# The mask of windowed attention added by a matmul with the identity instead of by VectorE

## The reference, cut to what matters

```
s_loc = einsum(q * scale, keys of 3 blocks)          # 128 queries x 384 keys
s_ctx = einsum(q * scale, context keys)              # 128 x 256
mask  = (|si - 128 - qi| <= 128) & (0 <= kpos < n)
s_loc = where(mask, s_loc, -inf)
p     = softmax(concat(s_loc, s_ctx, sink))
out   = p[:, :384] @ values of 3 blocks + p[:, 384:640] @ context values
```

## Time and profile before

| | us |
|---|---|
| median of 3 runs | 3833.14 |
| lowest, highest | 3831.15, 3833.17 |
| profiled execution, its own time | 3832.59 |
| its span in the profile | 3830.8 |
| TensorE busy in the span | 3366.6 |
| VectorE busy in the span | 1906.8 |

### The profile page before, as it was taken

The page is one execution under the profiler, slowest core; times in us unless marked ns, Lnnn a source line. Parts: engine busy times, 40 slices in busy tenths (PEclk is TensorE's granted clock), DMA queues, the critical chain, the costliest instruction groups (busy, mean ns, idle before and its releaser), DMA issues. The chain is left out here.

```text
span 3830.8 us, 47701 instructions
## 1 busy us (share of the span) xinstructions
PE 3366.6 (88%) x17144; PEld 2788.7 (73%) x17144; DVE 1906.8 (50%) x2918; ACT 847.1 (22%) x1570; POOL 1386.0 (36%) x1032
## 2 busy tenths in 40 slices
PE   0969989887979999999997669989787799999997
PEld 0848878755858888888884548878666578888885
DVE  8988533678582222222228888534675532222125
ACT  1136432212031010000003226432211121010102
POOL 1354213243324333343432253212242344444443
PEclk9979999978989999999998789999988899999998
DMA  7400001002301111011101510011002111111111
GB/s 276 170 17 1 1 29 60 12 20 85 121 28 39 39 38 38 33 44 39 35 30 67 176 55 1 0 39 50 12 14 80 39 39 49 49 49 50 44 49 49
DMA packets 63856, 197.72 MB, mean 52 GB/s; under 512 B 6160, under 2 KB 16656, under 8 KB 62736
## 3 DMA queue, kind: packets, MB, share of 16 engines
q1 hardware_dynamic: 54736, 172.32, 13.1%
q10 hardware_dynamic: 9024, 24.14, 1.7%
HBM read 177.05 MB, written 19.40 MB: 51 GB/s over the span
## 5 line engine op out<-in xcount | busy, mean ns | idle before, releaser
L188 PE MATMUL ps<-h_hi,f_whi 128*128 128x512 f32 (+1 forms) x1760 | 650.8, 370 | 27.0 <-DVE h_lo L1914 20.0
L189 PE MATMUL ps<-h_lo,f_whi 128*128 128x512 f32 (+1 forms) x1760 | 649.9, 369 | 0.0
L190 PE MATMUL ps<-h_hi,f_wlo 128*128 128x512 f32 (+1 forms) x1760 | 649.0, 369 | 0.0
L2142 DVE TENSOR_TENSOR f_gated<-f_gated,ps 128x512 f32<-128x512 f32 (+1 forms) x110 | 69.6, 634 | 973.8 <-PE ps L190 968.5
L2026 POOL TENSOR_TENSOR f_whi<-f_wraw,small 128x1024 fp32r<-128x1024 f32 x128 | 252.0, 1969 | 607.9 <-PE ps L190 607.9
L2150 DVE SCALAR_TENSOR_TENSOR x_res<-ps,mod,x_res 128x512 f32<-128x512 f32 (+1 forms) x440 | 306.8, 697 | 242.2 <-PE ps L190 242.0
L188 PEld LDWEIGHTS ps<-h_hi,f_whi 128*128 128x128 f32 x1760 | 333.2, 189 | 86.2 <-issue 22.7
L190 PEld LDWEIGHTS ps<-h_hi,f_wlo 128*128 128x128 f32 x1760 | 333.1, 189 | 55.7
L189 PEld LDWEIGHTS ps<-h_lo,f_whi 128*128 128x128 f32 x1760 | 333.4, 189 | 55.2
L188 PE MATMUL ps<-f_ahi,f_whi 128*128 128x512 f32 (+1 forms) x880 | 328.2, 373 | 0.0
L189 PE MATMUL ps<-f_alo,f_whi 128*128 128x512 f32 (+1 forms) x880 | 323.6, 368 | 0.0
(11 more groups left out here) (216 smaller groups left out, 6223.7 us busy)
## 6 DMA issues: line engine op xcount, KB each, us to landing
f_wraw<-in_w_ffn SPq DMA_DIRECT2D x132, 512.0 KB, 3.2
ada_w<-in_w_ada SPq DMA_DIRECT2D x80, 512.0 KB, 3.3
wrawc<-in_w_in SPq DMA_DIRECT2D x26, 512.0 KB, 3.7
wrawab<-in_w_in SPq DMA_DIRECT2D x16, 512.0 KB, 4.2
wrawo<-in_w_out SPq DMA_DIRECT2D x16, 512.0 KB, 3.3
ada_w<-in_w_ada ACTq DMA_DIRECT2D x16, 512.0 KB, 4.3
x_res<-in_xT SPq DMA_DIRECT2D x8, 640.0 KB, 6.3
x_spill<-x_res ACTq DMA_DIRECT2D x8, 640.0 KB, 5.9
```

The lines of the kernel that those rows point to most:

```text
L188: pe.matmul(out, w_hi, h_hi, start=first, stop=False)
L189: pe.matmul(out, w_hi, h_lo, start=False, stop=False)
L190: return pe.matmul(out, w_lo, h_hi, start=False, stop=last)
L2142: dve.tensor_tensor(g, g, pl.bank(3 + c, tn), ALU.mult).then_inc(u_taken[c], 1)
```

## The change

Two tiles are added at 188 KB and 188.5 KB of the stage's memory: the identity and the three masks, both in float32r. ScalarE fills them once per layer by copies from the constants, between the rounding of the first keys and the first exponential. TensorE opens each local unit's window with a matmul of identity (weights) and mask (moving, 384 columns) that starts the accumulation; the score matmuls of the window then accumulate on it. VectorE's addition and its semaphore wait are gone. TensorE waits for the two copies ahead of unit 0 alone.

```diff
+    ident = pl.at(f"{tag}_ident", [P, P], F32R, kb=188)
+    masks = pl.at(f"{tag}_masks", [P, 3, 3 * P], F32R, kb=188.5)
+    mask_in = pl.sem(f"{tag}_mask_in")
...
-                    pe.matmul(out, q_two[:, w.h, :], hi, start=True, stop=False)
-                    mm = pe.matmul(out, q_pad[:, w.h, :], lo, start=False, stop=True)
+                    local = w.kind == "A" and place < 3
+                    if local and place == 0:
+                        if w.static and w.u == 0:
+                            pe.wait_ge(mask_in, 2)
+                        variant = 1 if not w.static else 0 if w.i == 0 else 2 if w.i == LT - 1 else 1
+                        pe.matmul(w.scores(0, 3), ident[:, :], masks[:, variant, :], start=True, stop=False)
+                    pe.matmul(out, q_two[:, w.h, :], hi, start=not local, stop=False)
+                    mm = pe.matmul(out, q_pad[:, w.h, :], lo, start=False, stop=not local or place + n == 3)
...
-                if w.kind == "A":
-                    if w.static:
-                        variant = 0 if w.i == 0 else 2 if w.i == LT - 1 else 1
-                    else:
-                        variant = 1
-                    win = w.scores(0, 3)
-                    dve.tensor_tensor(win, win, pl.c(MASKS + 3 * P * variant, 3 * P), ALU.add) \
-                        .then_inc(masked, 1)
-                    dve.wait_ge(masked, w.u + 1)
...
             round_keys(0)
+            act.activation(ident[:, :], pl.c(IDENT), ACT.Copy).then_inc(mask_in, 1)
+            act.activation(masks[:, :, :].rearrange("p v k -> p (v k)"), pl.c(MASKS, 9 * P), ACT.Copy) \
+                .then_inc(mask_in, 1)
             exponent(Unit(0, 0, 0))
```

## The result

| | before | after |
|---|---|---|
| median, us | 3833.07 (6 runs) | 3812.89 (6 runs) |
| lowest to highest, us | 3831.15 to 3833.46 | 3806.95 to 3815.01 |
| profiled execution, us | 3832.59 | 3815.01 |
| its span, us | 3830.8 | 3813.2 |

The ratio after to before is 0.9948, with a 95% interval of 0.9938 to 0.9959: 20.2 us less in the median, 17.6 in the span of the profiled executions. A second series gave 3813.07 against 3832.03, ratio 0.9957 (0.9943 to 0.9971). I had forecast 3825.2 us, 7.9 less, in a range that ended at 3820.

What follows compares the result with a forecast made beforehand. The bound was taken as a cycle through TensorE and VectorE in the local attention units. Steps saving 9.5 us, less 1.6 lost at stage starts, gave 7.9 us off the median: 3825.2 us, range 3820 to 3833.

Steps and rivals of the forecast that it cites:

- What bounds the kernel: Local attention units: a cycle through TensorE and VectorE, 5.31 us for two units, the addition 0.60 of it.
- M: TensorE's cost of one added mask matmul of 384 columns: 0.175 us taken, bounds 0.16 and 0.26.
- rival 1: Mask matmul on TensorE: identity's load or opener's gap is paid, M = 0.26, saving 2.0 us, 3831.1 us; chance 0.15.
- The 53 steps: Unit-to-unit steps of both layers' local units at 2.4 GHz: 129.9 us against 139.3, 9.5 us saved.
- The copies at nothing: ScalarE's two added copies per layer: costed at nothing, at most their 1.4 us per layer.
- Start of each stage ... Net 1.6 us lost: Early units of each layer's attention: masks cost 16 M = 2.8 us, exposed first additions give 1.2 us back.
- One unit earlier or later in each layer is worth 3.3 us either way, and I can't tell which: TensorE's clock rise among each layer's early units: a one-unit shift is worth 3.3 us, direction unknown.
- The main case: The forecast itself, whole kernel: 7.9 us saved, 3825.2 us; chance 0.50.
- Rival 3: Early attention units: clock rises a unit earlier in both layers as TensorE idles less, 3.3 us more saved, 3821.9; chance 0.17.
- Rival 2: Local units: TensorE binds already and the addition was covered, so masks cost 12.1 us, 3845.2 us; chance 0.06.
- Rival 4: Ahead of the transposes: small waits of 0.08 us per unit stay, 4.2 us given back, 3829.4 us; chance 0.12.

Runs made afterwards that it cites:

- the narrow mask: Changed kernel with the mask matmul over the outer two key blocks only (256 columns instead of 384), put behind the window's score matmuls: 3814.4 us, ratio 0.9948.
- experiments 8 and 10: 8: the narrow mask, 3814.4 us; 10: kernel before with the mask matmul in layer 0 alone, run once more, 3822.44 us.
- experiments 5 and 11: Kernel before with unused matmuls in TensorE's waits: 5, 8 at each layer's start and 4 ahead of unit 2's scores, 3827.01 us; 11, the 4 alone, 3825.43 us.
- experiment 3: Changed kernel with VectorE's addition kept beside the mask matmul, so the window is masked twice: 3835.98 us, ratio 1.0009.
- experiments 5 and 6: Unused matmuls (8 plus 4) in TensorE's first waits of each layer's attention: 5, in the kernel before, 3827.01 us; 6, in the changed kernel, 3813.7 us.

## Why the prediction was wrong, point by point

- **What bounds the kernel: right.** The cycle of 5.31 us through the addition held. Four kernels fit it within 0.04 us per unit: 2.74 computed and 2.71 measured with both operations, 2.44 and 2.43 for the change, 2.36 and 2.35 with neither, 2.41 and 2.41 with the narrow mask. For the change itself TensorE's bare turn gives the same 2.44, so there the two can't be told apart.
- **M: right.** 0.175 taken, 0.18 measured, with the opener's gap shifted as described. The identity's load is not paid: it starts at 281.35, beside the value matmuls (280.74 to 281.57) ahead of the mask matmul at 281.38. The doubt of rival 1, and the higher estimate from the Trainium skill ("TensorE: Matmul & The Clock Gate", on the back-to-back issue gap and on LDWEIGHTS), is refuted for this width by the 0.18.
- **The 53 steps: right,** 129.9 forecast and 129.8 measured.
- **The copies at nothing: right.** They took 1.46 us per layer and TensorE was released by GpSimd as before.
- **"Start of each stage ... Net 1.6 us lost": wrong.** I charged TensorE's masks at half clock in full, 0.8 us per layer on balance, and returned one addition. In layer 0, where the clock rose alike, the stretch to unit 4 shrank by 0.25 us instead of growing by 0.6. The step from unit 1 to 2 fell from 6.77 to 6.32: unit 2's scores and its addition follow a wait of TensorE (2.14 us), so more than the first addition was exposed. That is 0.9 us per layer mis-sized, and with the ends of the local units (0.3 and 0.5 us, which I had not counted) 2.6 us together.
- **"One unit earlier or later in each layer is worth 3.3 us either way, and I can't tell which": this is the step that failed, with the largest term.** The main case put the clock's part of the saving at nothing: a coin beside the change, with equal sides and one unit of reach. In layer 1 it rose two units sooner, an estimate of 4.5 us there (layer 1's attention fell by 9.9 us, layer 0's, where the clock rose alike, by 5.4). The coin also looks tilted: early rises were seen only without the addition, and at the same place relative to the clock's fall (in experiments 8 and 10 at the same place in time as well). Rival 3 had the sign and the reason, at 0.17 and 3.3 us; it should have been joined to the main case. Its form was not met: one layer moved by two units, the other not at all. That TensorE's idle time is the cause in this stage is shown by experiments 5 and 11. That the removed addition acts through it is the likeliest reading and is not shown: TensorE's wait ahead of the first transposes fell from 1.48 to 0.56 us, but a single added or removed wait of that size was not tried.
- **Other stages: not counted.** They gave 2.3 us in the profiled pair, with unchanged code; over all profiles they took 3280.2 to 3288.7 us apart from the kernel before (3289.2), and how long their clock is low differs too. The range had no term for that: it took the 2 us spread of three runs of the kernel before, where 24 runs later went from 3820 to 3835.
- **Rival 2 (covered addition): refuted** by experiment 3. **Rival 4 (a new wait):** 0.2 us ahead of the transposes, refuted.

The sum in the profiled pair: 7.9 forecast, 0.1 more by the rate, 2.6 for starts and ends, 4.5 for the clock in layer 1 and 2.3 in other stages make 17.4 of the 17.6 us. The medians are 20.2 apart; the last 2.6 us belong to no trace. At equal clock the change is worth an estimated 11 us where the clock rises late (twice layer 0's 5.4) and about 13 where it is up from the start (experiments 5 and 6), so even without the clock's move 7.9 was too little. How the rest divides stays open. In part it is luck, as the same binary rose at 14.1 and at 8.6; in part it is probably the change, as no stage with the addition rose early.

## What to carry to other kernels

Write the cycle of two alternating buffers out from starts in the trace, with each engine's bare turn beside it: here that gave the new rate to 0.01 us before the change was run. Moving work from an engine inside the cycle to TensorE pays as long as TensorE's bare turn stays under the old rate. At a stage's start it may pay again, if a TensorE with fewer waits gets its full clock sooner; give that a term and a range of its own, and check it with a filler in both kernels. When differences are a few microseconds, compare the edited stages with each other, and the stages with unchanged code too, before comparing totals: here a gain of 3.4 us in the total was none in the stage.

## What the runs showed of the hardware

- In this kernel the clock's rise after a stage's start is as large as many edits: with the same binary, layer 0's attention took 275.7 and 273.2 us in two profiles, at rises of 14.1 and 8.6 us.
- Useless matmuls in a wait went with a faster kernel (3825.43 against 3832.03 us); the clock rose 6 to 13 us earlier in the two stages with them.
- A matmul of identity times 384 mask columns added 0.18 us to TensorE's turn at 2.4 GHz (0.86 instead of 0.68 from its start to the transposes), where VectorE's addition over the same 384 columns in PSUM took 0.57.
- Leaving a mask away altogether gained nothing measurable in the total over adding it on TensorE (3813.78 and 3812.89 us, in different series), although its step was 0.09 us shorter.
